# A four-layer conv and mLSTM trunk: short-conv groups that alternate, PSUM banks by last use, respaced modulation blocks, reordered mLSTM steps

## The reference

```
cond = silu(c)
for layer in range(4):
    sh1, sc1, g1, sh2, sc2, g2 = split(cond @ ada_w[layer] + ada_b[layer], 6)
    h = rms_norm(x) * (1 + sc1) + sh1
    layers 0, 2:  gb, gc, u = split(h @ w_in, 3);  y = (gb * conv3(gc * u)) @ w_out
    layers 1, 3:  q, k, v, o, i, f = split(h @ w_in)
                  y = (per-head norm(mlstm(q, k, v, i, f)) * sigmoid(o)) @ w_out
    x = x + (1 + g1) * y
    h = rms_norm(x) * (1 + sc2) + sh2
    g, val = split(conv3(h @ w_up) + b, 2)          # w_up is 1024 x 5632
    x = x + (1 + g2) * ((silu(g) * val) @ w_down)   # w_down is 2816 x 1024
return rms_norm(x)
```

## Time and profile before

| | |
|---|---|
| median of 3 runs | 3117.84 us (3116.27 to 3283.32) |
| the profiled execution | 3113.84 us |
| its span, first to last instruction, slowest core | 3112.2 us |
| TensorE busy | 2904.9 us (93%) |
| VectorE busy | 2037.2 us (65%) |
| ScalarE busy | 1211.0 us (39%) |
| GpSimd busy | 1010.1 us (32%) |
| cores, spans | 3090.8 to 3112.2 us |
| TensorE clock, mean | 0.983 to 0.989 of full speed |
| weights' DMA queue | 256 MB, 56.5% of 16 engines |

### The profile page before, as it was taken

How to read it: one execution, slowest core, us unless ns; L and a number is a source line. 1 busy time by engine, 2 the same in 40 slices (tenths; PEclk the granted TensorE clock), 3 DMA queues, 4 the chain that set the end, 5 groups by cost and what they waited for, 6 DMA issues and landing times.

```text
span 3112.2 us, 45790 instructions; the slowest of 8 cores (3090.8 to 3112.2 us)
## 1 busy us (share of the span) xinstructions
PE 2904.9 (93%) x15696; PEld 1361.1 (44%) x15696; DVE 2037.2 (65%) x2752; ACT 1211.0 (39%) x1907; POOL 1010.1 (32%) x898
## 2 busy tenths in 40 slices
PE   1898998999998999999999899999999899999997
PEld 0343444444454544444443344444445454444443
DVE  0567675786665557678667577668756465766876
ACT  2322353353453425335332225425425252542541
POOL 1312153154152515315330305405414242440540
PEclk9999999999999999999999999999999999999999
DMA  9884577676706266666773445765753425555443
GB/s 191 117 114 63 77 106 107 97 109 92 105 15 96 31 94 99 101 103 98 105 106 54 68 74 86 109 105 82 111 86 55 72 38 84 79 78 78 74 71 121
DMA packets 271859, 276.51 MB, mean 89 GB/s; under 512 B 9104, under 2 KB 267408, under 8 KB 271632
## 3 DMA queue, kind: packets, MB, share of 16 engines
q0 software_dynamic: 266592, 256.00, 56.5%
q1 hardware_dynamic: 5040, 17.57, 1.8%
HBM read 521.15 MB, written 8.39 MB: 170 GB/s over the span
## 4 chain that ended last, share of the span: by engine, by line
PE 78%; DVE 8%; DMA 5%; issue 4%; ACT 2%; POOL 2%; DVEq 0%; ACTq 0%; POOLq 0%
PE ps L228 77%; DVE work L201 4%; DVE work L191 2%; DMA ring<-ffn_w_down 2%; ACT work L188 2%; DMA ring<-ada_w 2%; DMA ring<-ml_w_out 1%; POOL work L194 1%; DVE work L207 1%; POOL h_sb L215 1%; PE ps L237 1%; DVE x_sb L201 0%; DVE halo_pr L211 0%; ACT L188 0%; DVEq L252 0%
## 5 line engine op out<-in xcount | busy, mean ns | idle before, releaser
L228 PE MATMUL ps<-h_sb,ring 128*128 128x512 bf16 x8192 | 1807.3, 381 | 47.2 <-DVE work L191 40.4
L228 PEld LDWEIGHTS ps<-h_sb,ring 128*128 128x128 bf16 x8192 | 793.7, 98 | 1009.5 <-issue 81.7
L201 DVE SCALAR_TENSOR_TENSOR work<-ps,params_sb,work 128x1023 bf16<-128x1023 f32 x704 | 902.1, 1281 | 280.5 <-ACT halo_u L188 162.4
L228 PE MATMUL ps<-work,ring 128*128 128x512 bf16 x3840 | 855.5, 385 | 54.4 <-DMA ring<-ml_w_out 15.8
L194 POOL TENSOR_TENSOR work<-work 128x1024 bf16<-128x1024 bf16 (+2 forms) x344 | 588.2, 1721 | 401.0 <-ACT work L188 370.4
L188 ACT ACTIVATE work<-ps,params_sb 128x1024 bf16<-128x1024 f32 x352 | 423.4, 1203 | 651.5 <-PE ps L228 651.5
L201 DVE SCALAR_TENSOR_TENSOR x_sb<-ps,mods,x_sb 128x512 f32<-128x512 f32 x512 | 384.0, 750 | 394.3 <-PE ps L228 378.7
L228 PEld LDWEIGHTS ps<-work,ring 128*128 128x128 bf16 x3840 | 377.5, 99 | 516.7 <-issue 82.3
L188 ACT ACTIVATE h_sb<-work,mods 128x512 bf16<-128x512 f32 x192 | 138.1, 722 | 438.1 <-DVE work L201 353.1
L188 ACT ACTIVATE work<-ps 128x512 bf16<-128x512 f32 (+3 forms) x352 | 179.5, 520 | 237.2 <-PE ps L228 219.8
L242 POOL DMA_DIRECT2D ring<-ffn_w_up x96 | 87.8, 914 | 554.9 <-PE ps L228 554.9
(11 more groups left out here) (62 smaller groups left out, 1065.8 us busy)
## 6 DMA issues: line engine op xcount, KB each, us to landing
ring<-ffn_w_up POOLq DMA_DIRECT2D x80, 1024.0 KB, 9.9
ring<-ada_w POOLq DMA_DIRECT2D x48, 1024.0 KB, 13.4
ring<-ffn_w_down POOLq DMA_DIRECT2D x32, 1024.0 KB, 10.0
ring<-sc_w_in POOLq DMA_DIRECT2D x24, 1024.0 KB, 11.1
ring<-ml_w_in POOLq DMA_DIRECT2D x24, 1024.0 KB, 11.1
ring<-ffn_w_down POOLq DMA_DIRECT2D x16, 768.0 KB, 9.1
x_sb<-xT SPq DMA_DIRECT2D x16, 512.0 KB, 16.9
ring<-sc_w_out POOLq DMA_DIRECT2D x8, 1024.0 KB, 11.0
```

The lines of the kernel that those rows point to most:

```text
L201: return self.op("dve", lambda e: e.scalar_tensor_tensor(out=out, in0=in0, scalar=scalar, in1=in1, op0=op0, op1=op1), reads, [out])
L228: return self.op("pe", lambda e: e.matmul(out, lhsT=lhsT, rhs=rhs, start=start, stop=stop), [lhsT, rhs], [out], mark=mark)
```

## The change

- **Short conv** (`shortconv_phase`): the blocks are now two "a" blocks and one "b" block per half of the features. An "a" block holds 256 columns of `gc` and the same 256 of `u` (`wblock_two`: two DMAs with a semaphore each). Per feature there are two `gc` groups, then two `u` groups, then one `conv3` over 1024 columns. The "b" block is `gb` as before. Hosted steps: at every second group of "a" and every group of "b"; in the very first phase at every group from the 11th. The square adds move to VectorE (`dve_sum=True`), the apply steps stay on ScalarE there (`pool_add=ml`).
- **Banks**: `next_bank` and `next_pair` give the bank, or pair, that was handed out longest ago. The mLSTM reports its fixed banks with `touch`.
- **Modulation blocks**: layer 0's last two go from its first MLP half to its second short-conv half. In the MLP they follow blocks 2, 4, 6, 8, 14 and 16.
- **mLSTM**: while k is projected one hosted step runs per group, not two; in all chunks, not only the first two, two run at the end. In the lead-in the first value group stands before the scores. The output group in the middle of chunk 0 is left out and stands before the numerator of chunk 7. Each of the two `b_v` slots is released right after its last value group. The hooks follow groups 1, 3, 5, 7 of `outproj` instead of 2, 4, 6, 8.

The diff, cut to its core. In the loop of `shortconv_phase` the removed lines are left out (they are printed above):

```diff
+        ring2_sem = [S.dma_sem("ringb%d" % i) for i in range(NS)]
...
-            S.dma("pool", ring[:, s, 0:kc, 0:ncols], src, ring_sem[s], writes=[ring[:, s, :, :]])
+            if isinstance(src, tuple):
+                for n, part in enumerate(src):
+                    cs = slice(n * ncols, (n + 1) * ncols)
+                    S.dma("pool", ring[:, s, 0:kc, cs], part, (ring_sem, ring2_sem)[n][s], writes=[ring[:, s, :, cs]])
+            else:
+                S.dma("pool", ring[:, s, 0:kc, 0:ncols], src, ring_sem[s], writes=[ring[:, s, :, :]])
             state["issued"] += 1
...
+        def wblock_two(w_ap, c0s, n):
+            src = tuple(w_ap[0:D, c0:c0 + n].rearrange("(kc p) n -> p kc n", p=128) for c0 in c0s)
+            blocks.append((src, D // 128, n))
             return len(blocks) - 1
...
         PAIRS = (0, 2, 6)
-        pair_rr = [0]
+        bank_use = {b: -1 for b in range(8)}
+        bank_n = [0]
+
+        def touch(b):
+            bank_n[0] += 1
+            bank_use[b] = bank_n[0]
 
         def next_pair():
-            b = PAIRS[pair_rr[0]]
-            pair_rr[0] = (pair_rr[0] + 1) % len(PAIRS)
+            b = min(PAIRS, key=lambda p: max(bank_use[p], bank_use[p + 1]))
+            touch(b)
+            touch(b + 1)
             return b
 
         def next_bank():
-            b = BANKS[bank_rr[0]]
-            bank_rr[0] = (bank_rr[0] + 1) % len(BANKS)
+            b = min(BANKS, key=lambda p: bank_use[p])
+            touch(b)
             return ps[:, b, :]
...
-            def __init__(self, hf, gm_ap=None, sh_ap=None, dve_sum=False):
+            def __init__(self, hf, gm_ap=None, sh_ap=None, dve_sum=False, pool_add=False):
...
-                            self.b.append(lambda t2=t2, c=c: apply_step(hf, t2, c, gm_ap, sh_ap, dve_sum))
+                            self.b.append(lambda t2=t2, c=c: apply_step(hf, t2, c, gm_ap, sh_ap, pool_add))
...
-        def conv3(dst, src, o, w_cols, bias_col):
+        def conv3(dst, src, w_cols):
             w0, w1, w2 = w_cols
-            if bias_col is None:
-                S.ts(dst, src[:, o + 2:o + 2 + TT], w2, None, ALU.mult)
-            else:
-                S.ts(dst, src[:, o + 2:o + 2 + TT], w2, bias_col, ALU.mult, ALU.add)
-            S.stt(dst, src[:, o + 1:o + 1 + TT], w1, dst, ALU.mult, ALU.add)
-            S.stt(dst, src[:, o:o + TT], w0, dst, ALU.mult, ALU.add)
+            n = HALF
+            S.ts(dst, src[:, 2:2 + n], w2, None, ALU.mult)
+            S.stt(dst, src[:, 1:1 + n], w1, dst, ALU.mult, ALU.add)
+            S.stt(dst, src[:, 0:n], w0, dst, ALU.mult, ALU.add)
...
+            naj = [4]
+
+            def with_ada(entry):
+                aj = naj[0] if first else None
+                if li == 0 and hf == 1 and naj[0] in (5, 8):
+                    aj = 10 + (naj[0] == 8)
+                naj[0] += 1
+                seq.append(entry + (aj, None if aj is None else ada0[0](aj)))
             for i in range(2):
-                for n, (kind, c0) in enumerate((("gc", D), ("u", 2 * D), ("gb", 0))):
-                    bi = wblock(w_in, 0, D, c0 + 512 * i, 512)
-                    aj = 4 + 3 * i + n if first else None
-                    seq.append((kind, i, bi, aj, ada0[0](aj) if first else None))
+                for a in range(2):
+                    f0 = 4 * i + 2 * a
+                    with_ada(("a", f0, wblock_two(w_in, (D + f0 * 128, 2 * D + f0 * 128), 256)))
+                with_ada(("b", 4 * i, wblock(w_in, 0, D, 512 * i, 512)))
...
-                for kind, i, bi, aj, abi in seq:
+
+                def tick(kind):
+                    ngrp[0] += 1
+                    if ngrp[0] > 10 if first else kind != "a" or ngrp[0] % 2 == 0:
+                        side.tick_b()
+                for kind, f0, bi, aj, abi in seq:
                     slot = use_block(bi)
...
+                    if kind == "a":
+                        for m2 in range(2):
+                            f = f0 + m2
+                            m = f % 4
                             halo_in(sc_pr[:, m, 0:2], halo_pr[:, f, :], hf)
...
+                            for t2 in range(2):
+                                hs = slice(t2 * TT, (t2 + 1) * TT)
+                                pb_ap = next_bank()
+                                S.group(pb_ap, wchunks(slot, m2), hcols(hf, hs))
                                 S.act(sc_gc[:, m, hs], pb_ap, AF.Copy)
...
+                                tick("a")
+                            for t2 in range(2):
+                                pb_ap = next_bank()
+                                S.group(pb_ap, wchunks(slot, 2 + m2), hcols(hf, slice(t2 * TT, (t2 + 1) * TT)))
+                                S.tt(sc_pr[:, m, 2 + t2 * TT:2 + (t2 + 1) * TT], pb_ap, sc_gc[:, m, t2 * TT:(t2 + 1) * TT], ALU.mult)
+                                tick("a")
+                            conv3(sc_cv[:, m, :], sc_pr[:, m, :], [pcol(pb + P_MIX + jj * 8 + f) for jj in range(3)])
+                            S.copy(halo_pr[:, f, :], sc_pr[:, m, 1024:1026])
+                    else:
+                        for m in range(4):
+                            for t2 in range(2):
+                                hs = slice(t2 * TT, (t2 + 1) * TT)
+                                pb_ap = next_bank()
+                                S.group(pb_ap, wchunks(slot, m), hcols(hf, hs))
+                                S.tt(yb_sc[:, f0 + m, hs], pb_ap, sc_cv[:, m, hs], ALU.mult)
+                                tick("b")
                     done_block(bi)
                     if abi is not None:
                         ada0[1](aj, abi)
+                        if aj == 11:
+                            ada0[2](40, 48)
                 if first:
                     ada0[2](16, 40)
                 outproj(wo, hf, md, side, lambda k, t2: yb_sc[:, k, t2 * TT:(t2 + 1) * TT])
...
             todo = []
-            if li == 0 and hf == 0:
-                todo += [(ada0, 10), (ada0, 11)]
             if ada_li is not None:
                 ada = ada_parts(ada_li[0])
                 todo += [(ada, ada_li[1] + n) for n in range(6)]
-            every = 2 if len(todo) > 6 else 3
+            spots = (2, 4, 6, 8, 14, 16)
             seq = []
             nblk = [0]
 
             def with_ada(entry):
                 nblk[0] += 1
                 extra = None
-                if nblk[0] % every == 0 and todo:
+                if nblk[0] in spots and todo:
                     a, aj = todo.pop(0)
                     extra = (a, aj, a[0](aj))
                 seq.append((entry, extra))
...
-                if a is ada0:
-                    if aj == 11:
-                        a[2](40, 48)
-                elif aj in (5, 11):
+                if aj in (5, 11):
...
                             side.tick_b()
-                            side.tick_b()
+                            if which == "q":
+                                side.tick_b()
...
                     pb_ap = ps[:, 6 + vb[0] % 2, :]
+                    touch(6 + vb[0] % 2)
...
                     pb_ap = ps[:, 6 + vb[0] % 2, :]
+                    touch(6 + vb[0] % 2)
...
                 nbf_step(0)
+                step_v(0, 0)
                 step_s(0)
+                step_v(0, 1)
                 step_k(0)
-                step_v(0, 0)
-                step_v(0, 1)
+                n_o = [0]
+
+                def o_group():
+                    step_o(n_o[0])
+                    n_o[0] += 1
                 for c in range(8):
                     if c < 7:
                         step_s(c + 1)
                         step_v(c + 1, 0)
+                        if c == 6:
+                            done_block(b_v[0])
+                    else:
+                        o_group()
                     step_num(c)
                     post_a(c)
-                    step_o(2 * c)
+                    if c > 0:
+                        o_group()
                     step_p(c, 0)
                     if c >= 4:
                         step_t(c - 4)
                     post_b(c)
                     if c < 7:
                         step_v(c + 1, 1)
+                        if c == 6:
+                            done_block(b_v[1])
                         step_k(c + 1)
                     step_p(c, 1)
                     post_c(c)
-                    step_o(2 * c + 1)
-                    if c == 6:
-                        for bi in b_v:
-                            done_block(bi)
-                    if c < 2:
-                        side.tick_b()
-                        side.tick_b()
+                    o_group()
+                    side.tick_b()
+                    side.tick_b()
                 for bi in b_o:
                     done_block(bi)
+                for b in (5, 0, 1, 2, 3):
+                    touch(b)
                 hooks = [(lambda c=c: step_t(c, (0, 1, 2, 3)[c - 4])) for c in range(4, 8)]
```

(6 more changed lines are left out.)

23 lines of the change are left out of this document (1 added, 22 removed).

## The result

The changed kernel takes **2970.07 us** (median of 4 runs) against 3117.84 before: ratio 0.9528, 95% interval 0.9501 to 0.9556, so 147 us less. The profiled execution took 2969.86 us with a span of 2968.3 (cores 2962.2 to 2968.3); by spans the gain is 143.9 us. The forecast was 2990 and 128; the measured time lies 2 us under its own case (2972 to 3015) and inside the wide range (2965 to 3042). The direction, the three sources and the way in which each works were as predicted; the size was too small. In some executions one die ran at a lower granted clock; ratios and intervals leave those out, and where too few were left I give spans only.

What follows compares the result with a forecast made beforehand. The prediction held that a busy TensorE is already fast, so only its gaps can be won: 55 (short conv) + 38 (feed-forward) + 35 (mLSTM) = 128 us, from 3117.8 to 2990 us; own case 2972 to 3015, wide range 2965 to 3042.

Steps and rivals of the forecast that it cites:

- A: Short conv: TensorE gaps of 61.2 us in all, of which 55 us were forecast to be won.
- rival (1): Short conv: VectorE becomes the bound, 7.5 us per feature against 6.9; A gives 25 to 30, about 3018 us; chance 0.11.
- (2): Loads stay late in short conv or feed-forward; A loses 15 to 22, B half: 3025 to 3031 us; chance 0.11.
- (5): Short conv: split loads are paced per row rather than by bytes, so the kernel is slower, 3182 us at 28 us each; chance 0.03.
- B: Feed-forward: 39.2 us of gaps, 38 forecast to be won; lower end 15 if only banks help.
- (e): mLSTM output projection: a 1.15 us wait goes (4.6 us), but the bank order brings waits of 1.26 and 1.00; net 0.
- C: mLSTM, four phases: waits counted one by one, 35 us to be won, between 20 and 42.
- (b): mLSTM lead-in: the mask product stands behind 4 hosted steps instead of 12; 12 of 12.9 us go.
- (d): mLSTM chunk ends: hosted steps in chunks 0 to 5 instead of 0 and 1 cost 2 us, upper end 7.
- (a): mLSTM: early slot release ends the ml_w_out load waits (15.8 us) and the slow start after them (5.0), 20.8 us.
- (c): mLSTM chunk 7: the moved output group covers the waits for the numerator's evictions, 4.3 us.
- Rival (4): Whole kernel: bank order is the rotation renamed and the waits only move; 3056 us, within 2%; chance 0.08.

Runs made afterwards that it cites:

- e5: Changed kernel with the short conv's square adds back on GpSimd: 2970.92 us, ratio 0.9525.
- e7: Changed kernel with short-conv groups in rows again (unsplit blocks) and the square adds back on GpSimd: 3005.9 us, ratio 0.9637.
- e8: Changed kernel with banks that rotate as before: span 2982.4 us, ratio 0.9568.
- e2: Kernel before with PSUM banks by last use alone: span 3109.4 us, 2.8 us won.
- e16: Changed kernel with modulation blocks after blocks 3, 6, 9, 12, 15 and 18 in all MLP halves: 2989.62 us, ratio 0.958.
- e3: Kernel before with modulation blocks alone respaced (2, 4, 6, 8, 14, 16; layer 0's last two in its second short-conv half): span 3096.6 us.
- e4: Kernel before with the mLSTM part alone (early release, lead-in, hosted steps, output groups), banks rotating: span 3058.0 us, ratio 0.9778.
- e13: Changed kernel with the mLSTM's hosted steps as before (two per k group, chunk ends only in chunks 0 and 1): span 2986.4 us, ratio 0.9577.
- e15: Changed kernel with output groups as before (one mid chunk 0, none before chunk 7's numerator): 2978.84 us, ratio 0.9545.
- e9: Changed kernel with both value slots released late, after the output group of chunk 6, as before: 2996.61 us, ratio 0.961.
- e14: Changed kernel with the mLSTM lead-in in the old order (scores, transposed keys, then value groups): span 2970.6 us.
- e10: Changed kernel with hook transposes on the longest-unused bank, a chunk 7 output group after `step_p(7, 0)`, MLP hosted steps from the first down group: 2954.51 us.

## Why the prediction was right in kind and short in size

**The yardstick held.** "Nothing but its gaps can be won": short conv and MLP now have no gap, and the MLP half of layer 3 that was the yardstick took 228.4 us.

**Short conv, A.** Forecast 55 of 61.2; measured 60.3 in its windows and 62.1 alone. Two terms were too cautious. The convolution over 1024 columns was priced at 3.5 us between 3.0 and 3.9; it takes 0.48 + 2.67 = 3.15, near the lower end of 3.0. And the 5 us kept back, 2 of them for the loads, were not needed. VectorE after, on one feature without hosted adds:

```profile
91.27 0.69 DVE L191 TENSOR_TENSOR work<-ps,work 128x512 bf16<-128x512 f32 x1 [1.05 <-PE ps L228]
92.07 0.48 DVE L207 TENSOR_SCALAR work<-work,params_sb 128x1024 bf16<-128x1024 bf16 x1
92.66 2.67 DVE L201 SCALAR_TENSOR_TENSOR work<-work,params_sb 128x1024 bf16<-128x1024 bf16 x2
```

It waits for TensorE before each product here, and still 0.95 us before the second one of a feature with hosted adds: rival (1), VectorE as the bound, fell. The predicted 90 us of VectorE per phase were 76.7 and 77.8. The shares of the causes, from e5 to e7: the order of the groups 18.6 us, the adds 1 us with it and 18 without. The remaining 24 or so of A (61 less 36.6) may be the wide convolution, but two other edits stand in e7 as well and none was tried apart: the new spacing of the hosted steps, and the banks by last use, which are worth 1.8 us here (e8).

**The loads.** The share rule held: 0.91 was predicted for the first phase, 0.94 measured, without a wait. The half blocks landed later than the 5.8 us of the earlier trace rows, since the second of a pair stands behind the first, but there was room. DMA issues after (KB each, median us to landing), then the group of GpSimd's issues of sc_w_in (busy us, mean ns):

```profile
ring<-sc_w_in POOLq DMA_DIRECT2D x32, 512.0 KB, 9.9
ring<-sc_w_in POOLq DMA_DIRECT2D x8, 1024.0 KB, 11.4
```

```profile
L242 POOL DMA_DIRECT2D ring<-sc_w_in x40 | 35.0, 876 | 300.2 <-PE ps L228 300.2
```

Rivals (2) and (5) fell. An issue takes 0.88 us, as before. The Trainium skill's rule (SBUF — State Buffer, "Who interferes with whom") that VectorE's two-port modes hold up GpSimd's descriptors would have shown in these loads first; no run here shows it.

**Feed-forward, B.** Forecast 38, measured 42.1, or 40.5 without the moved blocks, beside 39.2 recoverable by my count. Both mechanisms showed. I had said that banks alone would give 15; e2 gave 2.8. The lower end overlooked that a load that is late takes up the time a bank gives. But in the MLP stages alone e2 gave 8.1; the other 5 went in the mLSTM, whose loss from these banks the prediction had counted in (e) and left out of this lower end. Undone from the full change the two edits are worth 17.3 us (e8) and 19.1 (e16) in the MLP stages, 14.1 and 19.5 in the span. So the banks are worth twice as much once the loads are in time, while respacing is worth no more with the banks than without (25.4 in e3, though e16 does not restore the old positions of layer 0).

**mLSTM, C: the step that failed.** Forecast 35, measured 45.1 (49.4 alone, e4). Of the 19.5 us by which the windows' 147.5 exceed the forecast, 10.1 are here, more than in A and B together. The four phases, cut at the first value group of chunk 1 and the second one of chunk 7, and at the first matmul of the output projection (us in sum, slowest cores). One output group per phase, 6.9 us in sum, moved from the second row to the third and is counted back:

| stretch of a phase | before | after | won | forecast |
|---|---|---|---|---|
| gates, q, k and lead-in | 154.7 | 143.0 | 11.7 | 10: (b) 12, (d) -2, with the next row |
| chunks up to v(7,1) | 244.8 | 234.1 | 3.8 | |
| v(7,1) to the output projection | 64.2 | 48.3 | 22.8 | 20.1: waits of (a) 15.8, (c) 4.3 |
| output projection | 134.4 | 127.6 | 6.8 | 5.0: slow start of (a) 5.0, (e) 0 |

First, (b) and (d): 15.5 against 10. The loss of 2 us booked as (d), for hosted steps in more chunks, does not exist: a chunk with two steps at its end lasts as long as one without (8.96 us in the changed kernel and in e13), and this stretch became 3.8 us shorter, some 2.3 of it the slow clock that the prediction had in (b). And the first row won 11.7 us, while its waits by their rows fell by 8.7 only (from 11.0 to 2.4). Second, (c): undone alone it costs 6.2 us in these phases (e15), not 4.3, since its two short waits are each followed by slower matmuls. Third, in all rows, a wait was priced at what its row says, which the prediction named as some 0.2 us short and then used only as an upper end. The rows below show it: from eight transposes to the next matmul it is 0.45 us without a wait (892.33 to 892.78) and 1.76 with one of 1.15 (896.23 to 897.99), so 1.31 are lost. There were 32 waits in the four phases and are 18. In e9 and e13 a lower rate that costs 1.6 to 1.9 us stands behind every one of the eight long waits; I had priced it only where the trace of before showed it.

The terms undone one by one, in the four phases: (a) 29.0 us against 20.8 (e9, slowest core; 13 to 17 on its four quicker ones), (b) with (d) 18.8 and 0.5 against 10 (e13, e14), (c) 6.2 against 4.3 (e15). They sum to 54.5, more than the 45.1, since e13's lead-in is worse than the old one was (2.67 us in every phase, 1.6 in layer 1 before), and e9 sets a late load where TensorE now comes earlier (waits of 20.0 us, 15.8 before).

(e) is where the prediction was sharpest. Banks 6, 7, 5, 0, 1, 2, 3 put a wait before the sixth group and before the last transposes, in all four phases: all eight came. The price of this bank order, 4.5 us by the prediction, is 3.7 by e8, whose output projections take 123.9 us instead of 127.6. That the earlier hooks win 4.6 was not tried apart. TensorE after, against the last rows:

```profile
884.66 0.46 PE L228 MATMUL ps<-work 128*128 128x256 bf16 x6 [0.69 <-DVE work L201]
...
892.33 0.61 PE L237 MATMUL ps<-ident_bf,work 128*128 128x128 bf16 x8
892.78 3.62 PE L228 MATMUL ps<-work,ring 128*128 128x512 bf16 x16
896.23 0.61 PE L237 MATMUL ps<-ident_bf,work 128*128 128x128 bf16 x8
897.99 3.61 PE L228 MATMUL ps<-work,ring 128*128 128x512 bf16 x16 [1.15 <-DVE work L191]
902.61 0.61 PE L237 MATMUL ps<-ident_bf,work 128*128 128x128 bf16 x8 [1.00 <-DVE x_sb L201]
```

e10 takes the fixed banks away and moves an output group before the first of them, and all three are gone.

**Rivals (3) and (4)** fell: the mLSTM gives nothing back, and no load or bank wait returned elsewhere. Rival (4) had a grain of truth, but only for a part alone: in e2 and e3 part of the waits moves, to the late loads and to the mLSTM.

## What to carry to other kernels

Read a change by stages, not by the span alone: the banks alone won 2.8 us, which was 8.1 won in the MLP and 7.8 lost in the mLSTM, and a load that was late at the same point hid half of their worth in the MLP (17.3 once it was in time). Look at all cores: a late load cost core 5 of e9 29 us and its neighbour, core 4, 17. Price a gap of TensorE by the time until it is back at full rate, not by the wait's row: here 4.3 us for 2.67. And spread the slower engine's work evenly: in alternating order GpSimd's adds stretched VectorE's passes less often (4.5 against 16.7 us) and the slack took what was left (1 us lost against 18).
